# Rope rotation, key halves and tail norms moved from TensorE to VectorE and ScalarE in a two-block fp32 kernel

## The chip, the cores and the metric

One Trainium2 chip, one core. The metric is the device time of one launch in microseconds (us). Three runs of the kernel before gave a median of 1538.11 us (1537.73 to 1539.76).

## What is computed

The reference is a stack of two blocks on a sequence of 256 rows, D = 1024, in fp32. The first block has feed-forward layers, a recurrent mixer and a spatial gating mixer. The second block has two hybrid layers; each one computes projections of the normed input, sliding-window attention with 16 heads of 64 channels (two key heads, 16 meta tokens, so L = 272), and an mLSTM. The change lies in the attention's queries and keys:

```python
def rms_norm_2(x, g):
    y = xf * lax.rsqrt(jnp.mean(xf * xf, axis=-1, keepdims=True) + EPS)
    return (y * g.astype(jnp.float32)).astype(x.dtype)

def apply_partial_rope(x, cos, sin):
    half = ROT_DIM // 2                                   # ROT_DIM = 16
    x1, x2, rest = x[..., :half], x[..., half:ROT_DIM], x[..., ROT_DIM:]
    out = jnp.concatenate([x1 * c - x2 * s, x2 * c + x1 * s, rest], axis=-1)
...
scores = jnp.einsum('bnqkgd,bnskd->bnkgqs', qb, kb) * scale    # q, k normed per head, then rotated
e = jnp.exp(scores - m)
probs = e / (e.sum(axis=-1, keepdims=True) + jnp.exp(sink_b - m))
```

## The kernel before

Five instruction streams are written by hand, one for each engine, and run in the order in which they are written; semaphores tie them together.

**Weights.** The weights stream through in units of up to four 128x256 blocks in a ring of four slots. For each unit SyncE starts a load of 512 KB into `raw`, ScalarE makes `w_hi` (line 951, a rounded copy), VectorE makes `w_lo = raw - w_hi` (line 1478), and TensorE runs three products for each block (lines 541 to 543: hi·hi, hi·lo, lo·hi) on two output tiles, so 24 matmuls for a unit. `split_w(U + 3)` stands at unit U in ScalarE's and VectorE's streams: weights are made three units ahead. `w_hi` of unit U can be written once TensorE has finished unit U - 4. VectorE then takes each output tile from its bank with `scaled` (line 1518).

**Attention between the units.** In each hybrid layer the steps of the attention are hung on units by the table `VISITS`: TensorE does them after the unit of that number, VectorE and GpSimd at the same place in their streams. The phases are kv (units 0, 1), mif (2, 3), aq (4 to 11), mqk (12 to 19), and then the rest. The steps that matter here:

- `turn(c)`, c = 0 for the keys and 1 to 8 for the query chunks (two heads of 64 channels in the 128 partitions), at unit 5 (c = 0) and two each at units 7, 9, 11 and 13. ScalarE squares the chunk (line 1159). GpSimd multiplies it by sine and cosine tables (lines 1439 and 1440; `qs`, `qc`, two buffers each). TensorE sums the squares by head (line 733, into bank 4) and rotates `qs` with the matrix `rot_g` (line 738, into bank 5 or 6). VectorE adds that bank to `qc` (line 1842). `turn_mm` is raised by line 738, and ScalarE's next squares and VectorE's addition wait for it.
- `rs` at unit 14: VectorE turns the sums of squares into reciprocal roots (lines 1832 to 1835, `norms`), a chain of small steps that ends with `rs_new`.
- `rt` at units 15 and 16: TensorE waits for `rs_new`, transposes `norms` (line 757), ScalarE copies it to `r_t`, TensorE spreads it by one-hot matrices over the partitions of each head (line 747 for the keys, line 750 for the last 16 rows of eight chunks). VectorE scales the keys (line 1848) and the tail queries (line 1851, into `q_tail`).
- `kx` at unit 17: TensorE swaps the two key halves of 64 partitions by a matrix (line 763), transposes the values (765) and gate rows (770). ScalarE copies the swapped halves to `k_swap` and `k_up` (1168, 1169), VectorE the unswapped half and the values (1860 to 1867).
- `att` from unit 18: one head a visit. Line 801 is the first score matmul (the tail item of a key head), and it waits for all that `kx` made.

Matmuls of plain fp32 operands (lines 733 to 763) run in two passes, and so the profile has two records for each.

Of the kernel before, what the change touches and what calls it, by code (L numbers as in the profile page):

```python
# [38 lines left out]
CONST_W = dict(ident=P, tri=P, amask=AW, tmask=L, mmask=P, rot=P, swap=P, head_mean=2, cos=L, sin=L, sel=(NC8 + 1) * P)  # L39
# [8 lines left out]
def constants():  # L48
# [13 lines left out]
    for h0 in (0, DH):  # L62
        for d in range(half):
            c["rot"][h0 + half + d, h0 + d] = -1
            c["rot"][h0 + d, h0 + half + d] = 1
    c["swap"][i, (i + DH) % P] = 1
# [4 lines left out]
    for h0 in (0, DH):  # L71
        for k in (0, half):
            c["cos"][h0 + k:h0 + k + half] = np.cos(ang)
            c["sin"][h0 + k:h0 + k + half] = np.sin(ang)
    for k in range(NC8 + 1):
        for e in range(2):
            c["sel"][2 * k + e, k * P + e * DH:k * P + (e + 1) * DH] = 1
# [15 lines left out]


# [77 lines left out]
def build_stack(nc: bass.Bass, consts, x, ffn1_norm, ffn1_w_in, ffn1_w_out, mix_norm, ffn2_norm, ffn2_w_in, ffn2_w_out,  # L172
# [12 lines left out]
    with ExitStack() as ctx:  # L185
# [80 lines left out]
        rot_g = region(2, P)  # L266
# [1893 lines left out]
```

## Time and profile before

| | us |
|---|---|
| median of three runs | 1538.11 |
| the profiled execution | 1541.56 |
| its span in the trace | 1539.8 |
| TensorE busy | 1488.7 (97%) |
| VectorE busy | 1050.3 (68%) |
| ScalarE busy | 768.7 (50%) |
| GpSimd busy | 293.7 (19%) |

All times below are microseconds from the span's start. Layer 0's `turn` to `kx` lies between 980 and 1042, layer 1's between 1269 and 1329. The profiled execution lies 3.45 us above the median of the timed runs.

### The profile page before, as it was taken

The page shows a single profiled execution, that of the slowest core. Times are in us where ns is not written, and L with a number is a line of the kernel's source. Part 1 is how long each engine was busy: PE and PEld are TensorE (multiplying, and loading weights), DVE is VectorE, ACT ScalarE, POOL GpSimd, SP SyncE. Part 2 cuts the span into 40 slices and gives each one's busy share as a digit, 9 for nine tenths or more (in the row PEclk, how much of TensorE's full clock was granted, in tenths as well). Part 3 has the DMA queues.
Part 4 walks back from the last instruction along what each step waited for, and adds up shares of the span by engine and source line. Part 5 has one row for each costly group of instructions (what it writes and reads, how often), then busy time and mean ns, then how long its engine had stood idle before and what let it go on. Part 6 is the DMA issues. An engine that isn't in the chain of part 4 may idle for free.

```text
span 1539.8 us, 31458 instructions
## 1 busy us (share of the span) xinstructions
PE 1488.7 (97%) x11949; PEld 1467.5 (95%) x11949; DVE 1050.3 (68%) x2004; ACT 768.7 (50%) x1276; POOL 293.7 (19%) x361
## 2 busy tenths in 40 slices
PE   7999998999999999999999998999999999999998
PEld 7999998999999999999999997899999999899898
DVE  6666578766655666557766655888768768976883
ACT  5444458554545554454554534446744453566442
POOL 4111112211111111113311112343200125331000
PEclk9999999999999999999999999899999999999999
DMA  6656744555555655555565554443333554334333
GB/s 203 188 177 199 243 161 132 164 182 176 184 175 185 191 178 179 170 184 165 163 188 176 179 180 126 126 120 97 97 111 109 164 139 137 101 106 117 109 121 121
DMA packets 245276, 239.66 MB, mean 156 GB/s; under 512 B 15160, under 2 KB 244392, under 8 KB 245048
## 3 DMA queue, kind: packets, MB, share of 16 engines
q1 hardware_dynamic: 245176, 238.29, 50.8%
q8 instruction: 67, 1.10, 0.3%
q14 instruction: 33, 0.27, 0.1%
HBM read 237.21 MB, written 1.05 MB: 155 GB/s over the span
## 4 chain that ended last, share of the span: by engine, by line
PE 85%; DVE 10%; ACT 2%; issue 2%; POOL 1%; DMA 0%; SPq 0%; DVEq 0%; ACTq 0%; POOLq 0%
PE bank L541 25%; PE bank L543 25%; PE bank L542 25%; DVE w_lo L1478 3%; PE bank L865 1%; PE bank L805 1%; PE bank L823 1%; PE bank L788 1%; ACT w_hi L951 1%; DVE work L1518 1%; DVE work L1633 1%; PE bank L871 1%; PE bank L881 1%; PE bank L804 0%; DVE rstd L1496 0%
## 5 line engine op out<-in xcount | busy, mean ns | idle before, releaser
L1478 DVE TENSOR_TENSOR w_lo<-raw,w_hi 128x1024 fp32r<-128x1024 f32 (+1 forms) x456 | 557.7, 1232 | 317.8 <-ACT w_hi L951 317.4
L541 PE MATMUL bank<-x_hi,w_hi 128*128 128x256 f32 (+1 forms) x2480 | 721.8, 291 | 7.1 <-DVE x_lo L1491 5.2
L543 PE MATMUL bank<-x_hi,w_lo 128*128 128x256 f32 (+1 forms) x2480 | 708.8, 286 | 0.0
L542 PE MATMUL bank<-x_lo,w_hi 128*128 128x256 f32 (+1 forms) x2480 | 708.3, 286 | 0.0
L951 ACT CAST w_hi<-raw 128x1024 fp32r<-128x1024 f32 (+1 forms) x456 | 466.2, 1031 | 273.5 <-PE bank L543 256.8
L541 PEld LDWEIGHTS bank<-x_hi,w_hi 128*128 128x128 f32 x2480 | 477.9, 193 | 10.3 <-issue 6.8
L542 PEld LDWEIGHTS bank<-x_lo,w_hi 128*128 128x128 f32 x2480 | 478.2, 193 | 1.0
L543 PEld LDWEIGHTS bank<-x_hi,w_lo 128*128 128x128 f32 x2480 | 477.5, 193 | 0.0
L541 PE MATMUL bank<-y_hi,w_hi 128*128 128x256 f32 (+1 forms) x1088 | 310.4, 285 | 8.4 <-DVE y_lo L1489 8.3
L543 PE MATMUL bank<-y_hi,w_lo 128*128 128x256 f32 (+1 forms) x1088 | 309.8, 285 | 0.0
L542 PE MATMUL bank<-y_lo,w_hi 128*128 128x256 f32 (+1 forms) x1088 | 309.7, 285 | 0.0
L541 PEld LDWEIGHTS bank<-y_hi,w_hi 128*128 128x128 f32 x1088 | 209.3, 192 | 9.4 <-DVE w_lo L1478 4.4
L543 PEld LDWEIGHTS bank<-y_hi,w_lo 128*128 128x128 f32 x1088 | 209.4, 193 | 0.0
L542 PEld LDWEIGHTS bank<-y_lo,w_hi 128*128 128x128 f32 x1088 | 209.2, 192 | 0.0
L1353 POOL TENSOR_TENSOR work<-work,rstd 128x256 f32<-128x256 f32 x88 | 63.6, 742 | 415.1 <-ACT work L987 415.1
L1518 DVE TENSOR_TENSOR work<-bank,rstd 128x256 f32<-128x256 f32 (+1 forms) x204 | 81.7, 422 | 17.1 <-PE bank L543 16.7
L997 ACT CAST y_hi<-work 128x256 f32 (+1 forms) x88 | 35.6, 408 | 90.3 <-DVE work L1534 90.2
L987 ACT ACTIVATE work<-work 128x256 f32<-128x256 f32 x88 | 36.1, 419 | 78.3 <-DVE work L1518 78.3
L1334 POOL TENSOR_TENSOR sq<-h 128x256 f32<-128x256 f32 (+1 forms) x48 | 33.5, 698 | 199.2 <-DVE h L1563 196.9
L958 ACT ACTIVATE x_hi<-h,par 128x256 fp32r<-128x256 f32 (+1 forms) x64 | 32.8, 514 | 70.2 <-DVE h L1563 62.7
L1491 DVE SCALAR_TENSOR_TENSOR x_lo<-h,par,x_hi 128x256 fp32r<-128x256 f32 (+1 forms) x64 | 36.3, 569 | 29.9 <-ACT x_hi L958 29.8
L1332 POOL TENSOR_TENSOR sumsq<-h 128x256 f32<-128x256 f32 (+1 forms) x8 | 4.9, 618 | 248.1 <-DVE h L1563 240.8
(269 smaller groups left out, 1250.4 us busy)
## 6 DMA issues: line engine op xcount, KB each, us to landing
raw<-in_ffn_w_in_dram SPq DMA_DIRECT2D x176, 512.0 KB, 3.7
raw<-in_w_in_dram SPq DMA_DIRECT2D x100, 512.0 KB, 3.6
raw<-in_ffn_w_out_dram SPq DMA_DIRECT2D x64, 512.0 KB, 4.2
raw<-in_w_out_dram SPq DMA_DIRECT2D x32, 512.0 KB, 3.8
raw<-in_ffn_w_out_dram SPq DMA_DIRECT2D x32, 384.0 KB, 3.1
raw<-in_rec_w_in_dram SPq DMA_DIRECT2D x16, 512.0 KB, 3.6
raw<-in_sg_w_in_dram SPq DMA_DIRECT2D x16, 512.0 KB, 3.5
raw<-in_rec_w_out_dram SPq DMA_DIRECT2D x8, 512.0 KB, 3.4
```

Source lines behind the costliest of these rows:

```text
L541: mm(acc, wh, xh, start=first and j == 0, stop=False)
L542: mm(acc, wh, xl, start=False, stop=False)
L543: i_ = mm(acc, wl, xh, start=False, stop=last and j == n - 1)
L951: nc.scalar.copy(w_hi[:, s, 0:n, :], raw[:, s, 0:n, :]).then_inc(hi_made, 1)
L958: i_ = activation(xview(dst, k, N), src, ACT.Copy, scale=scale)
L987: activation(ffn_s[:, m, :], ffn_t[:, m, :], ACT.Silu).then_inc(silu_done, 1)
L997: nc.scalar.copy(dst, ffn_h[:, m, :]).then_inc(act_hi, 1)
L1334: link(TT(sq[:, T0:L], src(c), src(c), MUL))
L1353: TT(ffn_r[:, m, :], ffn_s[:, m, :], rstd[:, META:L], MUL).then_inc(gate_scaled, 1)
L1478: TT(w_lo[:, s, 0:n, :], raw[:, s, 0:n, :], w_hi[:, s, 0:n, :].bitcast(fp32), SUB).then_inc(lo_made, 1)
L1491: i_ = STT(out=xview(dst_lo, k, N), in0=src, scalar=scale, in1=hi, op0=MUL, op1=SUB)
L1518: TT(dst, tile(pr, m, N), rstd[:, T0:L], MUL).then_inc(tile_read, 1)
```

## The change

For the rotation, GpSimd multiplies by a sine table that now holds the head's gain, the scale and the sign (`sin_g`, made by VectorE as `cos_g` is); VectorE then permutes the partitions of `qs` in place within each group of 32 (`stream_shuffle`, with `ROPE_SWAP` exchanging 0 to 7 with 8 to 15) and adds `qc`. Line 738's matmul and the banks 5 and 6 fall away there; TensorE's `turn` no longer waits for GpSimd, and the last matmul of the head sums raises `turn_mm`. In `rt`, the eight matmuls with 16 columns become one with 18 (`tail_rows`), from which VectorE makes a column of norms for each tail row (`tail_t`, `tail_r`); the tail queries are copied unscaled, and the norm becomes the scale of the exponential. In `kx`, VectorE copies the key halves across partitions, and both the swap matmul and ScalarE's two copies fall away.

```diff
 turn, TensorE
-                        mm(bank[4][0:w, at:at + 2], score[:, n % 2, a:a + w], cst("head_mean"), start=True, stop=True)
-                    pe.wait_ge(qc_new, n + 1)
-                    pe.wait_ge(cos_ready, l + 1)
-                    if c >= 2:
-                        pe.wait_ge(q_ready, n - 1)
-                    mm(bank[5 + n % 2][:, 0:L], rot_g[:, 0 if c else 1, :], qs[:, n % 2, :], start=True,
-                       stop=True).then_inc(turn_mm, 1)
+                        i_ = mm(bank[4][0:w, at:at + 2], score[:, n % 2, a:a + w], cst("head_mean"), start=True, stop=True)
+                    i_.then_inc(turn_mm, 1)
 rt, TensorE
-                        mm(bank[6][:, 0:L], con[:, at:at + P], r_t, start=True, stop=True)
-                        for c in range(NC8):
-                            at = CONST_AT["sel"] + (c + 1) * P
-                            i_ = mm(bank[7][:, c * TAIL:(c + 1) * TAIL], con[:, at:at + P], r_t[:, 2 * P:L],
-                                    start=True, stop=True)
-                        i_.then_inc(rt_mm, 1)
+                        mm(bank[6][:, 0:L], cst("k_rows"), r_t, start=True, stop=True)
+                        mm(bank[7][:, 0:NR], cst("tail_rows"), norms[:, 3, 2 * NR:3 * NR], start=True,
+                           stop=True).then_inc(rt_mm, 1)
                         return
                     pe.wait_ge(rs_new, l + 1)
-                    pe.wait_ge(q_ready, 9 * (l + 1))
+                    if l:
+                        pe.wait_ge(m_sb, M_H * l)
 kx, TensorE and ScalarE
-                    pe.wait_ge(k_ready, l + 1)
-                    mm(bank[4][:, 0:L], cst("swap"), k_att, start=True, stop=True)
-                nc.scalar.copy(k_swap[DH:P, :], bank[4][DH:P, 0:L])
-                nc.scalar.copy(k_up[0:DH, 1, :], bank[4][0:DH, 0:L]).then_inc(k_swapped, 1)
 att, ScalarE
-                            i_ = activation(pr[:, 0:L], s[:, 0:L], ACT.Exp, bias=nm[:, 0:1], accum_out=den[:, 0:1])
+                            i_ = activation(pr[:, 0:L], s[:, 0:L], ACT.Exp, scale=tail_r[:, g:g + 1], bias=nm[:, 0:1],
+                                            accum_out=den[:, 0:1])
 turn, GpSimd
-                    TT(qs[:, n % 2, :], src, cst("sin"), MUL)
+                    TT(qs[:, n % 2, :], src, sin_g[:, 0 if c else 1, :], MUL).then_inc(qs_new, 1)
 tables, VectorE
-                    TS(rot_g[:, 0, :], cst("rot"), gq, sc, MUL, MUL)
-                    TS(rot_g[:, 1, :], cst("rot"), gk, None, MUL).then_inc(cos_ready, 1)
+                    TS(sin_g[:, 0, :], cst("sin"), gq, sc, MUL, MUL)
+                    TS(sin_g[:, 1, :], cst("sin"), gk, None, MUL).then_inc(cos_ready, 1)
 turn, VectorE
-                    dve.wait_ge(turn_mm, n + 1)
-                    TT(dst, bank[5 + n % 2][:, 0:L], qc[:, n % 2, :], ADD).then_inc(q_ready, 1)
+                    dve.wait_ge(qs_new, n + 1)
+                    link(V.stream_shuffle(qs[:, n % 2, :], qs[:, n % 2, :], ROPE_SWAP))
+                    dve.wait_ge(qc_new, n + 1)
+                    dve.wait_ge(qsq_new, n + 1)
+                    TT(dst, qs[:, n % 2, :], qc[:, n % 2, :], ADD).then_inc(q_ready, 1)
 rt, VectorE
                     dve.wait_ge(rt_mm, 2 * l + 2)
+                    dve.wait_ge(q_ready, 9 * (l + 1))
                     TT(k_att, k_att, bank[6][:, 0:L], MUL).then_inc(k_ready, 1)
+                    link(TT(tail_t, bank[7][:, 2:NR], cst("tail_head"), MUL))
+                    link(V.tensor_reduce(tail_r[:, 0:2], tail_t.rearrange("p (g n) -> p g n", g=2), mybir.AxisListType.X, ADD))
+                    TS(tail_r[:, 2:4], tail_r[:, 0:2], -1.0, None, MUL)
-                            i_ = TT(q_tail[...], q[...], bank[7][...], MUL)
+                            i_ = V.tensor_copy(q_tail[...], q[...])
 kx, VectorE
+                    dve.wait_ge(padded, l + 2)
+                    dve.wait_ge(k_ready, l + 1)
+                    V.tensor_copy(k_swap[DH:P, :], k_att[0:DH, :])
+                    V.tensor_copy(k_up[0:DH, 1, :], k_att[DH:P, :])
+                    link(V.tensor_copy(k_up[0:DH, 0, :], k_att[0:DH, :]))
+                    V.memset(k_att[0:DH, :], 0.0).then_inc(k_swapped, 1)
                     dve.wait_ge(kx_mm, l + 1)
-                    dve.wait_ge(padded, l + 2)
-                    V.tensor_copy(k_up[0:DH, 0, :], k_att[0:DH, :])
...
-                    link(i_)
-                    V.memset(k_att[0:DH, :], 0.0)
```

VectorE's stream at units 7 and 8 of layer 0 before (`w_lo` of a unit is line 1478, tiles are line 1518, line 1606 is a step of the mLSTM's gate logarithm, line 1842 is the rotation's addition for two query chunks):

```order
L1478 TENSOR_TENSOR w_lo<-raw,w_hi 128x1024 x2
L1518 TENSOR_TENSOR work<-bank2,rstd 128x272
L1518 TENSOR_TENSOR work<-bank3,rstd 128x272
L1606 SCALAR_TENSOR_TENSOR work<-work 4x272 x4
L1842 TENSOR_TENSOR work<-bank6,work 128x272
L1842 TENSOR_TENSOR work<-bank5,work 128x272
L1478 TENSOR_TENSOR w_lo<-raw,w_hi 128x1024 x2
```

The same place after the change (the line numbers are the changed kernel's):

```order
L1466 TENSOR_TENSOR w_lo<-raw,w_hi 128x1024 x2
L1506 TENSOR_TENSOR work<-bank2,rstd 128x272
L1506 TENSOR_TENSOR work<-bank3,rstd 128x272
L1594 SCALAR_TENSOR_TENSOR work<-work 4x272 x4
L1830 STREAM_SHUFFLE work<-work 128x272
L1833 TENSOR_TENSOR work<-work 128x272
L1830 STREAM_SHUFFLE work<-work 128x272
L1833 TENSOR_TENSOR work<-work 128x272
L1466 TENSOR_TENSOR w_lo<-raw,w_hi 128x1024 x2
```

Two shuffles have come in ahead of the next weights, and the additions read SBUF alone.

VectorE's stream from `rt` to the first item of the attention, before (line 1922 is the mLSTM's convolution):

```order
L1848 TENSOR_TENSOR work<-work,bank6 128x272
L1851 TENSOR_TENSOR work<-work,bank7 64x64 x4
L1478 TENSOR_TENSOR w_lo<-raw,w_hi 128x1024
L1518 TENSOR_TENSOR pre<-bank0,rstd 128x272
L1518 TENSOR_TENSOR pre<-bank1,rstd 128x272
L1922 SCALAR_TENSOR_TENSOR work<-pre,par,work 128x272 x6
L1860 COPY work<-work 64x272
L1862 COPY work<-bank5 128x2x64 x2
L1862 COPY work<-bank5 16x2x64
L1865 MEMSET work 64x272
L1866 COPY work<-bank5 128x16
L1867 COPY work<-bank5 16x8
```

And after:

```order
L1840 TENSOR_TENSOR work<-work,bank6 128x272
L1841 TENSOR_TENSOR work<-bank7,con 128x16
L1842 TENSOR_REDUCE work<-work 128x2
L1843 TENSOR_SCALAR work<-work 128x2
L1846 COPY work<-work 64x64 x4
L1466 TENSOR_TENSOR w_lo<-raw,w_hi 128x1024
L1506 TENSOR_TENSOR pre<-bank0,rstd 128x272
L1506 TENSOR_TENSOR pre<-bank1,rstd 128x272
L1918 SCALAR_TENSOR_TENSOR work<-pre,par,work 128x272 x6
L1854 COPY work<-work 64x272
L1855 COPY work<-work 64x272
L1856 COPY work<-work 64x272
```

Three small instructions stand in `rt` ahead of the tail copies, and two more copies of 64x272 stand in `kx` ahead of the value copies.

## Rows read from the trace of the kernel before

**Rows 1.** The page: busy time, share of the span, instructions.

```profile
PE 1488.7 (97%) x11949; PEld 1467.5 (95%) x11949; DVE 1050.3 (68%) x2004; ACT 768.7 (50%) x1276; POOL 293.7 (19%) x361
```

**Rows 2.** Waits of TensorE: line, releaser: us in total, times, longest.

```profile
PE bank L757 <- DVE work L1835: 3.7, 2, 1.9
PE bank L738 <- DVE work L1518: 1.9, 1, 1.9
PE bank L738 <- POOL work L1440: 1.9, 2, 1.6
PE bank L801 <- issue: 1.6, 2, 0.8
```

**Rows 3.** Timeline, TensorE: start, us, line, tile, count of records.

```profile
1000.01 0.71 PE L738 MATMUL bank<-work 128*128 128x272 f32 x2
1000.56 0.65 PE L733 MATMUL bank<-con,work 128*128 128x2 f32 x6
...
1318.20 1.85 PE L750 MATMUL bank<-work,con 128*128 128x16 f32 x16
```

**Rows 4.** Windows: us; busy PE, PEld, DVE, ACT, POOL; granted clock; DMA, GB/s.

```profile
986.20:1026.04 39.84, 36.50 (x263) 35.33 (x261) 32.40 (x64) 13.29 (x19) 21.20 (x20) 0.91 0.42 119
1026.04:1041.80 15.76, 14.89 (x104) 13.97 (x105) 13.36 (x32) 7.80 (x14) 5.04 (x6) 0.89 0.35 101
1275.90:1314.13 38.23, 34.10 (x260) 32.93 (x259) 33.25 (x64) 13.09 (x19) 21.07 (x20) 0.96 0.43 125
1314.13:1328.40 14.27, 13.41 (x105) 12.52 (x105) 13.09 (x32) 7.80 (x14) 6.08 (x6) 1.00 0.39 110
1045.00:1140.00 95.00, 95.00 (x727) 92.32 (x726) 67.79 (x227) 58.87 (x160) 20.61 (x22) 1.00 0.39 111
```

**Rows 5.** Waits of VectorE between 986.20 and 1026.04.

```profile
DVE w_lo L1478 <- ACT w_hi L951: 5.5, 3, 3.6
DVE pre L1518 <- PE bank L543: 0.3, 1, 0.3
DVE work L1518 <- PE bank L543: 0.3, 1, 0.3
```

**Rows 6.** Waits of VectorE between 1275.90 and 1314.13.

```profile
DVE w_lo L1478 <- ACT w_hi L951: 3.4, 2, 2.1
```

**Rows 7.** Timeline of VectorE: single and linked operations of 272 elements.

```profile
1009.84 0.43 DVE L1823 TENSOR_TENSOR work<-work 4x272 f32<-4x272 f32 x1
1010.31 0.71 DVE L1824 TENSOR_TENSOR_SCAN work<-work 4x272 f32<-4x272 f32 x1
1011.73 0.77 DVE L1842 TENSOR_TENSOR work<-bank,work 128x272 f32<-128x272 f32 x2
1012.43 1.20 DVE L1478 TENSOR_TENSOR w_lo<-raw,w_hi 128x1024 fp32r<-128x1024 f32 x1
```

**Rows 8.** Timeline of VectorE: tables, weights beside GpSimd, `rt` and `kx`.

```profile
972.24 0.35 DVE L1793 TENSOR_SCALAR work<-con,par 128x272 f32<-128x272 f32 x1
972.50 0.36 DVE L1794 TENSOR_SCALAR work<-con,par 128x272 f32<-128x272 f32 x1
...
992.60 1.63 DVE L1478 TENSOR_TENSOR w_lo<-raw,w_hi 128x1024 fp32r<-128x1024 f32 x1
...
1033.52 0.44 DVE L1848 TENSOR_TENSOR work<-work,bank 128x272 f32<-128x272 f32 x1 [1.26 <-PE bank L750]
...
1040.36 0.28 DVE L1860 COPY work<-work 64x272 f32<-64x272 f32 x1
...
1041.59 0.14 DVE L1867 COPY work<-bank 16x8 f32<-16x8 f32 x1
```

**Rows 9.** Windows around pauses of TensorE; columns as in Rows 4.

```profile
989.50:996.30 6.80, 6.20 (x25) 5.97 (x26) 4.59 (x9) 0.86 (x2) 4.27 (x5) 0.50 0.62 173
1279.60:1283.00 3.40, 3.18 (x12) 2.95 (x13) 3.26 (x8) 0.78 (x2) 1.01 (x3) 0.50 0.83 256
1312.30:1314.20 1.90, 0.01 (x1) 0.02 (x2) 1.66 (x9) 0.00 (x0) 0.00 (x0) 1.00 0.17 58
1314.20:1318.00 3.80, 3.80 (x29) 3.52 (x30) 3.42 (x7) 2.33 (x4) 0.00 (x0) 1.00 0.41 110
```

More of the change, by code:

```diff
@@ L36 @@
 C_AQ, C_KV, C_AG, C_MQK, C_MV, C_MIF, C_MO, C_MG = 0, 1024, 1280, 2304, 3328, 4352, 4360, 5384
-CONST_W = dict(ident=P, tri=P, amask=AW, tmask=L, mmask=P, rot=P, swap=P, head_mean=2, cos=L, sin=L, sel=(NC8 + 1) * P)
+CONST_W = dict(ident=P, tri=P, amask=AW, tmask=L, mmask=P, head_mean=2, cos=L, sin=L, k_rows=P, tail_rows=P, tail_head=ATT_H)
 CONST_AT = {}
@@ L61, in constants @@
     half = ROT // 2
[L62 to L66, printed above, removed]
     c["head_mean"][i, i // DH] = 1.0 / DH
@@ L71, in constants @@
     for h0 in (0, DH):
-        for k in (0, half):
+        for k, sign in ((0, 1), (half, -1)):
             c["cos"][h0 + k:h0 + k + half] = np.cos(ang)
[L74 to L77, printed above, removed]
+            c["sin"][h0 + k:h0 + k + half] = sign * np.sin(ang)
+        c["k_rows"][h0 // DH, h0:h0 + DH] = 1
+    c["tail_rows"][i % TAIL, i] = 1
+    for g in range(2):
+        for j in range(4):
+            for e in range(2):
+                c["tail_head"][e * DH + j * TAIL:e * DH + (j + 1) * TAIL, 8 * g + 2 * j + e] = 1
     return np.concatenate([c[n] for n in CONST_W], 1)
@@ L92 @@
         _r += _k
+ROPE_SWAP = [*range(ROT // 2, ROT), *range(ROT // 2), *range(ROT, 32)]
 def plan():
@@ L265, in build_stack @@
         cos_g = region(2)
[L266 removed]
+        sin_g = region(2)
+        tail_r = region(1, 4)[:, 0]
+        tail_t = region(1, ATT_H)[:, 0]
         qsq = score[:, :, 0:L]
@@ L335, in build_stack @@
             sem(n) for n in ("ws_tr", "ws_read", "vt_tr", "vt_read", "sg_mm", "sg_read"))
-        cos_ready, qsq_new, qc_new, turn_mm, q_ready = (
-            sem(n) for n in ("cos_ready", "qsq_new", "qc_new", "turn_mm", "q_ready"))
+        cos_ready, qsq_new, qs_new, qc_new, turn_mm, q_ready = (
+            sem(n) for n in ("cos_ready", "qsq_new", "qs_new", "qc_new", "turn_mm", "q_ready"))
         rs_new, rt_mm, rt_read, k_ready, tail_new = (
@@ L1245, in nothing @@
                     return None
-                do = dict(turn=turn, rs=nothing, rt=lambda n: rt() if n == 0 else None, kx=lambda n: kx(), att=att,
+                do = dict(turn=turn, rs=nothing, rt=lambda n: rt() if n == 0 else None, kx=nothing, att=att,
                           silu=silu, mvt=mvt_chunk, ml=lambda hs: ml(*hs))
```

15 lines of the change are left out of this document (5 added, 10 removed).

## The prediction

> **What bounds the kernel now.** I read the busy times first: TensorE is busy 97% of the span [rows 1]. So matmuls that go away are worth their length, unless something else is late where they stood. The waits of TensorE name the places where something is: in the steps that the change touches it waits 3.8 us for what line 738 reads, 3.7 us ahead of `rt` for VectorE's root chain, and 1.6 us ahead of the first attention item [rows 2]. Then I cut the span into stages. In layer 0, from the first rotation's addition (986.2) to the end of the root chain (1026.04), TensorE has 36.5 us of work in 39.84 us and VectorE 32.4; in layer 1 it is 34.1 and 33.25 of 38.23 [rows 4]. The two engines are nearly even there, whereas in the attention that follows TensorE is busy all of 95 us and VectorE 68 [rows 4]. Both stretches end in one meeting point: TensorE's `rt` at unit 15 waits for `rs_new`, which VectorE raises at the end of a fixed stream. So the question of the first stretch is when VectorE gets there, not how much work TensorE has.
>
> **What TensorE sheds.** Line 738 takes 1000.56 - 1000.01 = 0.55 us until the next matmul can start, 18 of them 9.9 us; the sixteen 16-column records take 1.85 us and are replaced by two (0.23 us), twice, 3.2 us [rows 3]; the swap has line 738's form, at most 0.55 us, twice, 1.1 us. Together 14.2 us. Besides, the 3.8 us of waiting at line 738 go, and what followed them: the granted clock was 0.50, the 1.2 GHz level, for 6.8 us after the wait of 1.6 us in layer 0 and for 3.4 us after the 1.9 us in layer 1 [rows 2, 9], worth half of that, 5.1 us. That is 23.1 us in all, all of it ahead of the first attention item.
>
> **What VectorE takes on before `rs_new`.** Each of the nine chunks of a layer costs an addition now and a shuffle, a link and an addition after. A pair of unlinked additions lasts 0.77 us, 0.43 the single one, so 0.35 from start to start; a linked operation of 272 elements is followed after 1010.31 - 1009.84 = 0.47 us [rows 7]. No row is a shuffle. Its bounds: a one-source operation on 128x272 gives way after 0.26 us (972.24 to 972.50) [rows 8], with the link's 0.03 about 0.3 us; and 0.7 us if it is as long as the 0.47 of the linked operation, the two further waits cost something, and the addition, which now reads both inputs from SBUF, is stretched by GpSimd as line 1478 is (1.63 us beside it, 1.20 alone) [rows 7, 8]. I take 0.5 us, near the linked operation, since the operation is elementwise over the same 272. That is 4.5 us a layer. The two tables of 272 columns (0.26 us each) replace two of 128; I put the difference at 0.13 us a layer, half of one.
>
> By the Trainium skill, "VectorE: DVE Perf Modes", section "The perf-mode tier table", a stream shuffle has the 1x mode only, about 2400 ns for 2048 elements; an estimate from it is 0.32 us for 272. The Trainium skill, same page, section "The DRAIN you can't avoid", says that a semaphore after each operation costs nothing over none; the rows have 0.47 linked against 0.35 unlinked. With that rule the shuffle and its addition would add about 0.35 instead of 0.5 a chunk, and the whole result would be 2.7 us lower, 1539.2.
>
> **The first stretch.** How much can VectorE be pulled forward? Only by the time it now waits for others: 6.1 us in layer 0 [rows 5] and 3.4 us in layer 1 [rows 6]; almost all of it is for `w_hi`, which waits for a slot that TensorE frees. With TensorE ahead these waits go. So `rs_new` of layer 0 comes 6.1 - 4.5 - 0.13 = 1.5 us earlier, and that of layer 1 4.5 + 0.13 - 3.4 = 1.2 us later. TensorE meanwhile has, in layer 0, 36.5 us of work less 3.4 for the slow clock and 5.0 for nine matmuls, 28 us of a stretch of 38.3: it arrives some 10 us early at unit 15 and stands idle, and what it shed turns into a wait for VectorE at `rt`. GpSimd's part stays as it is; the chunk after next waits for `q_ready`, but VectorE comes back only two units later, and GpSimd needs 21 us of the 39 for all nine [rows 4].
>
> **From `rs_new` to the first item.** Behind `rs_new` VectorE has a fixed stream too: `w_lo`, tiles, convolution, `w_lo`, `rt`, `w_lo`, tiles, convolution, `kx`. In layer 0 it idles 1.26 us in it, for line 750 [rows 8]; the new `rt` needs TensorE 1.6 us less, so this goes. In layer 1 it is busy 13.09 of 14.27 us and has no such wait [rows 4]. Added: in `rt` a 16-column multiply, a reduction and a scalar step, all linked, about 0.15 us each (estimated from the small copy of 0.14 us [rows 8]), 0.45 us; in `kx` two more copies of 64x272 at 0.28 us each [rows 8], 0.55 us. So +1.0 us a layer, -1.3 in layer 0. ScalarE's two copies were beside other work and give nothing; the swap's matmul and the shorter `rt` lie in front of a wait and give nothing more. Layer 0: -0.3. Layer 1: +1.0.
>
> **The clock.** Now TensorE ends unit 18 about 15.0 us after `rs_new` in layer 0 and waits 0.8 us for the first item at 15.8 [rows 2, 4]. With `rt` 1.6 us and the swap some 0.5 us shorter it ends at 12.9, and the item can start at 15.5: a pause of 2.6 us. In layer 1 the same working gives 13.4 - 2.1 = 11.3 against 15.2, a pause of 3.9 us, or 2.2 if the clock was low behind `rt`. Pauses of 1.6 and 1.9 us ahead of line 738 were followed by 0.50 for 6.8 and 3.4 us; the one of 1.9 us ahead of line 757 in layer 1 was not (1.00 after it) [rows 2, 9]. A pause of 2.2 us or more is longer than all of these, so I take a period of 3.4 us at 1.2 GHz after it, 1.7 us, in each layer: +3.4 us. What follows is TensorE's own work [rows 4], so it counts in full. The ten idle microseconds ahead of `rt` will bring a slow period too. VectorE has 6.2 us of its own work between `rs_new` and `rt` (two weights, two tiles and a convolution), and TensorE at full clock needs some 4.3 for a unit and both halves of `rt`: a period of 3.4 us is hidden, one of 6.8 us (3.4 us lost) costs some 1.2 us a layer.
>
> **The sum**, against the profiled execution of 1541.56 us (span 1539.8, and 3.45 above the median): -1.5 + 1.2 - 0.3 + 1.0 + 3.4 = +3.8 us. On the median that is **1541.9 us**.
>
> **The rivals.**
> *The work comes off.* If VectorE has more room than its waits show, TensorE's 23.1 us come off, less the 3.4 us of the slow periods above and the 1.5 us in `rt` and `kx`: about 1520. For it speaks the share of TensorE in the whole span; against it that `rt` already waits for VectorE by 1.8 us in each layer before anything is shed. 7 in 100. Half-way, if the chunks cost 0.3 and the clock stays, -3.6 - 3.4 + 3.8 = -3.2, 1534.9, or somewhat below: 15 in 100.
> *No slow period ahead of the attention.* Then the sum is +0.4, 1538.5. The row of layer 1's `rt` speaks for it. Together with the case of cheap shuffles and slow periods (+0.2): 32 in 100.
> *VectorE and GpSimd stretch each other.* The mechanism: both inputs of the new addition come from SBUF, and the first chunk's `q_ready` sets GpSimd going on the next one while VectorE shuffles and adds the second. At 0.7 us a chunk `rs_new` comes 1.8 us later in each layer, +3.6 more, 1545.5; with slow periods of 6.8 us behind `rt` 1548. It is slower than before from 0.55 us a chunk on even if only one slow period comes. 16 in 100.
> *My forecast*, 1540 to 1544: 30 in 100.
>
> **How the numbers follow.** The likeliest is the forecast and gives the time. The range takes in the cheap end with the clock kept (1534.9, a little below) and the dear end (1548): 1534 to 1548. Left out is the case of the work coming off and the tails, about 15 in 100. Within 0.2% is 3.1 us to either side, about what a measurement here can tell: faster 0.18, same 0.36, slower 0.46; the forecast lies only 0.7 us beyond the bound, so a part of it counts as the same.
>
> **What would show it.** In the changed profile: TensorE's wait at the first transposes of `rt` is 8 to 11 us in both layers, on VectorE; VectorE's waits for `w_hi` between the first rotation and `rs_new` are close to none; from a shuffle's start to the next `w_lo` a pair takes about 1.7 us; the stretch corresponding to 986.20:1026.04 is about 38.3 us long, and layer 1's about 39.3; the wait ahead of the first item is 2.2 to 3.9 us, and the granted clock is 0.50 behind it. I am wrong if VectorE still waits for `w_hi` there, if the wait at `rt` is short, or if a shuffle takes far from 0.43 us.

## Result and profile after

The change makes the kernel slower: 1557.23 us (median of four, 1555.11 to 1557.53) against 1537.92 in the same session, a ratio of 1.0117 with a 95% interval of 1.0103 to 1.0132. The forecast was 1541.9 with a range of 1534 to 1548. Its sign and the two places where TensorE now waits for VectorE were right; the rise on the median was five times what was forecast (19.1 us for 3.8), because VectorE's added work was priced too low.

The page of the changed kernel (as [rows 1]; the span is 1555.5): TensorE is busy 8.5 us less, VectorE 19.3 more.

```profile
PE 1480.2 (95%) x11881; PEld 1459.5 (94%) x11881; DVE 1069.6 (69%) x2050; ACT 765.9 (49%) x1272; POOL 299.5 (19%) x361
```

TensorE's waits (line, releaser: us in total, times, longest), as [rows 2]. Line 752 is the first transpose of `rt`, 794 the first attention item, 544 the weight matmuls with `w_lo`.

```profile
PE bank L752 <- DVE work L1823: 19.1, 2, 9.5
PE bank L794 <- DVE work L1857: 8.6, 2, 4.6
...
PE bank L544 <- DVE w_lo L1466: 7.4, 5, 2.1
```

All three are VectorE's. The 3.8 us at the rotation's matmul [rows 2] are gone; these three have 15.4, 7.0 and 5.6 us more than before, 28 us in all (the wait for `w_lo` was 1.8). Of the waits for `w_lo` 5.0 us lie in the changed steps, 2.1 in layer 0 and 2.9 in layer 1.

Windows from the first shuffle to the end of the root chain in layers 0 and 1, then from there to the first attention item, as [rows 4] (us; busy PE, PEld, DVE, ACT, POOL; granted clock; DMA, GB/s):

```profile
988.00:1028.97 40.97, 29.37 (x242) 28.93 (x240) 39.22 (x81) 12.57 (x19) 24.16 (x20) 0.91 0.40 116
1283.99:1324.88 40.89, 28.50 (x238) 27.84 (x237) 39.15 (x81) 12.32 (x19) 24.20 (x20) 0.92 0.40 117
1028.97:1047.03 18.06, 14.03 (x88) 13.05 (x89) 15.94 (x37) 7.13 (x12) 6.74 (x8) 0.78 0.31 88
1324.88:1342.57 17.69, 12.99 (x89) 12.02 (x89) 16.44 (x37) 7.09 (x12) 6.79 (x8) 0.89 0.32 90
```

VectorE is busy 39.2 of 41 us where it was 32.4 of 39.8 and 33.3 of 38.2 [rows 4]. The time stands in this table, in us from each execution's trace. **B** goes from the layer's first head-sum matmul to the end of the root chain (`rs_new`), **C** from there to the first attention item; the columns between hold the rest.

| | start | B, layer 0 | C, layer 0 | to layer 1 | B, layer 1 | C, layer 1 | rest |
|---|---|---|---|---|---|---|---|
| before | 979.67 | 46.37 | 15.78 | 227.59 | 44.72 | 14.24 | 211.43 |
| the change | 981.30 | 47.67 | 18.06 | 230.27 | 47.58 | 17.69 | 212.93 |
| difference | +1.6 | +1.3 | +2.3 | +2.7 | +2.9 | +3.5 | +1.5 |

The differences add up to 15.7 us. One pair of chunks shows where B's come from. First VectorE's timeline in the changed kernel (1830 is the shuffle, 1833 the addition, 1466 `w_lo`, 1506 takes a tile from its bank), then GpSimd's products of the same moment:

```profile
994.26 0.46 DVE L1830 STREAM_SHUFFLE work<-work 128x272 f32<-128x272 f32 x1
994.75 0.44 DVE L1833 TENSOR_TENSOR work<-work 128x272 f32<-128x272 f32 x1
...
995.12 0.46 DVE L1830 STREAM_SHUFFLE work<-work 128x272 f32<-128x272 f32 x1
995.61 0.78 DVE L1833 TENSOR_TENSOR work<-work 128x272 f32<-128x272 f32 x1
996.32 3.50 DVE L1466 TENSOR_TENSOR w_lo<-raw,w_hi 128x1024 fp32r<-128x1024 f32 x2
999.75 0.77 DVE L1506 TENSOR_TENSOR work<-bank,rstd 128x272 f32<-128x272 f32 x2
```

```profile
995.34 0.76 POOL L1427 TENSOR_TENSOR work<-work 128x272 f32<-128x272 f32 x1 [2.92 <-DVE work L1833]
996.06 0.97 POOL L1428 TENSOR_TENSOR work<-work 128x272 f32<-128x272 f32 x1
996.99 1.75 POOL L1427 TENSOR_TENSOR work<-work 128x272 f32<-128x272 f32 x1
998.71 1.75 POOL L1428 TENSOR_TENSOR work<-work 128x272 f32<-128x272 f32 x1
```

The first addition has 0.44 us. It raises `q_ready` and lets GpSimd go. The second addition is issued at 995.61, in the middle of GpSimd's first product, and ends 0.34 us later than it would alone. Then the engines alternate, as worked out from these rows: GpSimd's second product ends at 997.03, the first `w_lo` about 1.04 us later (996.32 and half of 3.50), GpSimd's third at 998.74, the second `w_lo` 1.08 us after that (999.82), GpSimd's fourth 0.64 us later. Each runs while the other stands, and each record includes the standing. The shuffle beside GpSimd (995.12) and the tiles with one input from a bank (999.75) keep their lengths. `w_lo` goes from 1.41 and 1.45 us in the mean to 1.67 in both layers, ten times in each. Its group in the stretch from the first rotation to `rs_new` (total us and mean ns behind the bar, then VectorE's idle time in front of it), before and after, layer 0:

```profile
L1478 DVE TENSOR_TENSOR w_lo<-raw,w_hi 128x1024 fp32r<-128x1024 f32 x10 | 14.0, 1405 | 5.5 <-ACT w_hi L951 5.5
L1466 DVE TENSOR_TENSOR w_lo<-raw,w_hi 128x1024 fp32r<-128x1024 f32 x10 | 16.4, 1673 | 0.0
```

In C the same happens to copies. VectorE in the changed kernel, in layer 0 and (the last two lines) in layer 1: 1843 to 1846 belong to `rt`, 1854 to 1857 to `kx`; in layer 0 GpSimd runs products from 1034.17 to 1038.23 and from 1044.04 to 1047.30.

```profile
1036.81 0.60 DVE L1843 TENSOR_SCALAR work<-work 128x2 f32<-128x2 f32 x1
1037.32 1.39 DVE L1846 COPY work<-work 64x64 f32<-64x64 f32 x4
...
1043.94 0.30 DVE L1854 COPY work<-work 64x272 f32<-64x272 f32 x1
1044.25 0.76 DVE L1855 COPY work<-work 64x272 f32<-64x272 f32 x1
1045.03 0.82 DVE L1856 COPY work<-work 64x272 f32<-64x272 f32 x1
1045.96 0.28 DVE L1857 MEMSET work<- 64x272 f32 x1
...
1331.76 0.17 DVE L1843 TENSOR_SCALAR work<-work 128x2 f32<-128x2 f32 x1
1331.84 2.41 DVE L1846 COPY work<-work 64x64 f32<-64x64 f32 x4
```

The copy that starts ahead of GpSimd lasts 0.30 us, the next two 0.76 and 0.82. A step of two columns takes 0.60 us beside GpSimd (layer 0) and 0.17 alone (layer 1).

The pauses of TensorE in layer 0, from its timeline:

```profile
1029.03 0.72 PE L752 MATMUL bank<-con,work 128*18 128x128 f32 x3 [9.54 <-DVE work L1823]
...
1047.03 1.25 PE L794 MATMUL bank<-work 128*128 128x272 f32 x2 [3.98 <-DVE work L1857]
```

And the granted clock behind them, the third figure from the end, in windows of the changed kernel:

```profile
1030.00:1040.00 10.00, 10.00 (x63) 9.67 (x62) 8.57 (x20) 4.22 (x7) 3.90 (x4) 0.74 0.38 107
1040.00:1050.00 10.00, 6.02 (x35) 5.60 (x35) 7.99 (x21) 3.80 (x9) 3.10 (x4) 0.77 0.19 53
1047.03:1050.00 2.97, 2.97 (x11) 2.74 (x12) 1.65 (x4) 0.89 (x4) 0.27 (x1) 0.50 0.00 0
1050.00:1060.00 10.00, 10.00 (x71) 9.88 (x70) 7.30 (x23) 4.89 (x12) 1.75 (x2) 0.89 0.37 107
```

### The profile page after: what moved, and what is told of

The parts are those of the page before. It is cut to its first block, busy times and chain, and to the rows that moved or that the text cites. A ratio compares the mean times of both kernels' runs of the same rounds, so it can differ in the third digit from the quotient of the medians.

```text
span 1555.5 us, 31363 instructions
## 1 busy us (share of the span) xinstructions
PE 1480.2 (95%) x11881; PEld 1459.5 (94%) x11881; DVE 1069.6 (69%) x2050; ACT 765.9 (49%) x1272; POOL 299.5 (19%) x361
## 4 chain that ended last, share of the span: by engine, by line
PE 80%; DVE 14%; issue 2%; ACT 2%; POOL 0%; DMA 0%; SPq 0%; DVEq 0%; ACTq 0%; POOLq 0%
PE bank L544 24%; PE bank L546 24%; PE bank L545 24%; DVE w_lo L1466 4%; PE bank L858 1%; DVE work L1506 1%; PE bank L798 1%; PE bank L816 1%; DVE work L1918 1%; PE bank L781 1%; DVE work L1621 1%; ACT w_hi L944 1%; PE bank L864 1%; PE bank L874 1%; DVE work L1830 1%
```

## The experiments

Stages of each, in the columns of the table above:

| | start | B0 | C0 | to layer 1 | B1 | C1 | rest | ratio to before (95%) |
|---|---|---|---|---|---|---|---|---|
| rope alone | 979.21 | 47.69 | 16.68 | 227.81 | 47.60 | 15.81 | 211.30 | 1.0061 (1.0044 to 1.0078) |
| `kx` alone | 979.61 | 43.57 | 15.97 | 229.10 | 44.55 | 17.51 | 212.79 | 1.0036 (1.0022 to 1.0051) |
| tail norms alone | 980.64 | 45.12 | 15.94 | 229.16 | 44.49 | 15.93 | 212.82 | 1.0045 (1.0028 to 1.0062) |
| no shuffle | 980.22 | 43.75 | 17.67 | 230.63 | 42.95 | 17.73 | 213.65 | 1.0055 (1.0038 to 1.0072) |
| pauses filled | 980.88 | 47.67 | 17.67 | 227.87 | 47.58 | 17.68 | 211.35 | 1.0101 (1.0084 to 1.0117) |
| GpSimd 34 wide | 979.19 | 43.01 | 17.68 | 229.35 | 42.92 | 17.68 | 212.87 | 1.0042 (1.0026 to 1.0059) |
| `kx` on ScalarE | 979.39 | 47.66 | 16.38 | 229.42 | 47.54 | 16.02 | 212.89 | 1.0089 (1.0072 to 1.0106) |
| `qs` alone waited for | 979.73 | 42.37 | 15.78 | 227.56 | 42.18 | 14.24 | 211.54 | 0.9975 (0.9965 to 0.9985) |
| conv. behind norms | 980.97 | 43.36 | 22.21 | 229.18 | 43.26 | 22.20 | 213.72 | 1.0110 (1.0095 to 1.0125) |
| `qs` and conv. | 979.41 | 38.84 | 21.05 | 227.57 | 38.64 | 21.09 | 211.60 | 1.0011 (1.0002 to 1.0020) |
| GpSimd later | 980.08 | 47.12 | 17.70 | 230.64 | 47.08 | 17.73 | 212.95 | 1.0101 (1.0086 to 1.0117) |
| `qs`, GpSimd later | 980.78 | 44.10 | 15.76 | 227.60 | 43.87 | 15.78 | 211.51 | 1.0001 (0.9992 to 1.0010) |

The rows "no shuffle", "pauses filled", "GpSimd 34 wide", "`kx` on ScalarE", "conv. behind norms" and "GpSimd later" are edits of the changed kernel (itself 1.0117); the others are edits of the kernel before. A ratio of 0.001 is 1.5 us. The stages come from one profiled execution of each kernel, the ratios from all its runs.

### One part at a time

The rotation alone (its three hunks of the diff on the kernel before):

> The kernel before with the rotation alone moved to VectorE; tail norms and key halves stay on TensorE. Theory A (the VectorE stream ahead of rs_new is the path, and GpSimd lengthens it): most of the loss is here, +8 to +13 us over the kernel before, with a wait of 8 to 10 us at the first transposes of rt in both layers. Theory B (the key copies and the tail steps behind rs_new are the larger part): +2 to +5 us.

The key halves alone (`kx` hunks):

> The kernel before with the key halves alone copied by VectorE. Theory A: +3 to +5 us, as the two added copies take 0.76 and 0.82 us beside GpSimd in place of 0.28, in each layer, and the longer pause ahead of the first item brings a slow clock. Theory B (copies cost only what one alone costs): +1 us.

The tail norms alone (`rt` and exponential hunks):

> The kernel before with the tail norms alone changed: one matmul of 18 columns for eight of 16, unscaled copies, the norm as the exponential's scale. Theory A: VectorE gives back in layer 1 what TensorE saves in layer 0, -1 to +2 us. Theory B (TensorE's work comes off): -3 us.

The ratios say 9.4, 5.5 and 6.9 us (0.0061, 0.0036 and 0.0045 of 1540), 22 together; the change has 18. No part is worth having. The rotation's 9.4 us lie in the range of theory A, 5.5 us for `kx` a little above it. The rotation alone lengthens B to the change's own length in both layers, with TensorE waiting 9.5 and 8.1 us at `rt`. The tail norms missed both theories (-1 to +2, or -3): they take 1.6 us off TensorE ahead of `kx` and the first item comes no sooner. TensorE's waits between 1015 and 1055 in this kernel:

```profile
PE bank L803 <- issue: 4.1, 1, 4.1
PE bank L759 <- DVE work L1838: 1.8, 1, 1.8
```

In layer 0 the item started 15.78 us after `rs_new` before and starts 15.94 after it now, since VectorE sets it: its last copy of `kx` ends at 1041.60 and the item starts at 1041.70 (in layer 1, where it was 14.24, it is 15.93: the four copies of 64x64 last 2.40 us beside GpSimd, the multiplications lasted 0.92); TensorE only stands 4.1 us instead of 0.8, and the granted clock of 1040 to 1050 goes from 1.00 to 0.83, so that the stage behind it costs 1.6 and the last one 1.4 us more. `kx` alone has pauses of 3.0 us there and the same +1.5 and +1.4.

### The shuffle left out

```diff
-                    link(V.stream_shuffle(qs[:, n % 2, :], qs[:, n % 2, :], ROPE_SWAP))
```

> The changed kernel without the stream shuffle and its link (the sine products are added unpermuted, so the rotation is left out). The shuffle takes 0.46 us, 18 of them 8.3 us. If the VectorE stream sets the time of rs_new one for one and GpSimd's share is independent: 7 to 9 us faster than the changed kernel. If GpSimd's collision with the w_lo steps is what counts: 2 to 4 us faster only, with the two w_lo steps of a visit still at 3.5 us.

B shrinks by 3.92 and 4.63 us, 0.44 and 0.51 a chunk: the shuffle costs what its record says (0.458) and its link little. The ratio falls by 0.0062, 9.5 us, a little more than the 7 to 9 of the first theory. The pair of `w_lo` keeps its 3.50 us, so the hold is a cost of its own. B1, at 42.95, is 0.8 us longer than where TensorE's rotation doesn't wait (42.18), though TensorE has no rotation to do; likely this is the hold on additions and `w_lo`.

### The pauses filled

```diff
+                    for _ in range(15):
+                        mm(bank[6][:, 0:L], ident, x_hi[:, 0:L].bitcast(fp32), start=True, stop=True)
                     pe.wait_ge(rs_new, l + 1)
...
+                            for _ in range(6):
+                                mm(bank[4][:, 0:L], ident, x_hi[:, 0:L].bitcast(fp32), start=True, stop=True)
                             pe.wait_ge(k_swapped, l + 1)
```

> The change, with 15 extra fp32 matmuls of 272 columns in TensorE's stream ahead of its wait for rs_new and 6 ahead of its wait for att0's keys, in both layers; their results go into banks nobody reads. They only keep the array at work in the pauses (9.5 us ahead of rs_new, 4 to 4.6 us ahead of att0); all that is computed stays. Theory 'clock': the change's cost over its waits comes from the periods at 1.2 GHz that follow these pauses (granted clock 0.56 to 0.83 in 1020 to 1060 and 1310 to 1350); with the array busy they go, the stretch behind rs_new comes down from 18.1 and 17.7 us to about 16.5, att0 to the next layer's first norm matmul and to the end lose 1.5 to 2.5 us each, and the time falls by 5 to 9 us, to about 1548 to 1552, with mean clock at 0.99 instead of 0.981. Rival 'order': the clock only follows; VectorE's chain is the end in both places, so filling changes under 2 us (1555 to 1559). If the extra matmuls outlast a pause, the time rises instead and the chain of waits shows a shorter or no wait there.

Half right. The stages behind the items fall to the level of before (227.87 and 211.35), 2.40 and 1.58 us less than in the change: that is what the slow clock costs there. B doesn't move at all and C by 0.4 us, in layer 0 alone, so ahead of the items the slow clock costs next to nothing; it is VectorE that is late. (In layer 0 VectorE's wait of 0.86 us ahead of `rt` is gone too, but its steps there fall elsewhere against GpSimd's products, and the four copies of 64x64 take 2.40 us instead of 1.39.) The time fell by 2.5 us (0.0016 by the ratios), under the 5 to 9 expected; the 4.0 us of the two stages are from the fastest of its executions.

### GpSimd's products at 34 columns

```diff
-                    TT(qs[:, n % 2, :], src, sin_g[:, 0 if c else 1, :], MUL).then_inc(qs_new, 1)
+                    W = L if c < 2 else 34
+                    TT(qs[:, n % 2, 0:W], src[:, 0:W], sin_g[:, 0 if c else 1, 0:W], MUL).then_inc(qs_new, 1)
```

and the same for `qc`.

> The change, with GpSimd's two rotation products of chunks 2 to 8 made 34 columns wide instead of 272 (the other columns keep what the buffers held, so the rotated queries are not the reference's); VectorE's shuffles, additions, halves w_lo and all matmuls are as in the change. Theory 'GpSimd stretches VectorE': the second addition of a pair falls from 0.78 to about 0.44 us, the pair of w_lo from 3.50 to 2.4 to 2.8 us, a pair of chunks costs about 1.3 us less, four pairs 4 to 5 us a layer: first shuffle to rs_new 36 to 37 us instead of 41, TensorE's wait there 9.5 us falls to about 5, and the time falls by 8 to 12 us to about 1545 to 1549. Rival 'shuffle's own length and its links': additions and w_lo keep their lengths or VectorE waits for something else (w_hi, or the squares), and the time falls by less than 3 us.

VectorE's and GpSimd's timelines of this kernel, one pair:

```profile
999.98 0.50 DVE L1834 TENSOR_TENSOR work<-work 128x272 f32<-128x272 f32 x1
1000.40 2.41 DVE L1467 TENSOR_TENSOR w_lo<-raw,w_hi 128x1024 fp32r<-128x1024 f32 x2
```

```profile
999.70 0.26 POOL L1428 TENSOR_TENSOR work<-work 128x34 f32<-128x34 f32 x1 [3.75 <-DVE work L1834]
...
1000.62 1.11 POOL L1428 TENSOR_TENSOR work<-work 128x34 f32<-128x34 f32 x1 [0.44 <-DVE work L1834]
1001.69 1.24 POOL L1429 TENSOR_TENSOR work<-work 128x34 f32<-128x34 f32 x1
```

The pair of `w_lo` is back at 2.41 us, and a product of 34 columns that takes 0.26 us alone takes 1.11 beside a `w_lo`: now GpSimd is the one held. B falls by 4.66 us in each layer, and the ratio from 1.0117 to 1.0042, which is 11.5 us: both as expected. So of the change's cost in time more than half is VectorE standing while GpSimd works, with the clock behind it. TensorE's wait at `rt` is 7.3 and 8.3 us, not the 5 expected: its waits for `w_lo` in B (2.1 us in layer 0, 2.9 in layer 1) are gone too, so it comes earlier.

### The key halves copied by ScalarE

```diff
+                    nc.scalar.copy(k_swap[DH:P, :], k_att[0:DH, :])
+                    nc.scalar.copy(k_up[0:DH, 1, :], k_att[DH:P, :]).then_inc(k_swapped, 1)
...
-                    V.tensor_copy(k_swap[DH:P, :], k_att[0:DH, :])
-                    V.tensor_copy(k_up[0:DH, 1, :], k_att[DH:P, :])
```

> The change, with the two copies that make the swapped key halves moved from VectorE to ScalarE, straight from k_att (no swap matmul); the clearing of k_att waits for them. Theory 'VectorE's chain sets att0': rs_new to att0 is VectorE's own stream in the change (TensorE waits 4.0 and 4.6 us there); without the copies of 0.76 and 0.82 us it ends 1.3 to 1.7 us earlier in each layer, TensorE's pause falls to about 2.5 us, and with the clock the time falls by 3 to 6 us, to about 1551 to 1554. Rival 'shed work is the pause': the same stretch is set by something else (gate exponentials, w_hi), the pause stays at 4 us and the time moves by under 1.5 us. Third way: the copies on ScalarE delay w_hi there and att0 comes no sooner.

C falls by 1.68 and 1.67 us: the two copies' own length (0.30 and 0.76) and what the third was held, which falls from 0.82 to 0.29. VectorE's stream sets the first item. The ratio falls by 0.0028, 4.3 us, as expected.

### The first convolutions behind the norms

```diff
-                                if ph == "mqk":
+                                if ph == "mqk" and p:
                                     conv(p)
...
+                            if u == 14:
+                                conv(0)
```

> The change, with one edit of VectorE's order: the first pair of convolutions (six instructions of 128x272, 3.6 us where they stand, 12 scheduling groups before the attention) is done right behind the norms that raise rs_new instead of ahead of the last two rotation additions; nothing is computed otherwise. Theory 'VectorE's own stream sets rs_new, TensorE is only early': rs_new comes 2.9 to 3.6 us earlier in each layer, TensorE's wait there falls from 9.5 to about 6 us; but the convolutions then stand in the stretch from rs_new to att0, which VectorE sets too, so that this grows by as much (from 18.1 and 17.7 us to 20.5 to 21.5), TensorE's pause ahead of att0 grows from 4 to 4.6 us to 6 or more, and the time stays within 3 us of 1557. Rival 'only the wait at rs_new matters': rs_new to att0 stays at about 18 us and the time falls by 5 to 8 us.

B falls by 4.3 us in both layers, C rises by 4.2 and 4.5, and the ratio is 1.0110 for 1.0117. The gain in B was larger than the 2.9 to 3.6 expected, and so was the loss in C. TensorE's two waits in layer 0 become 5.23 and 6.93 us instead of 9.54 and 3.98, with one of 1.65 between them:

```profile
1024.39 0.72 PE L752 MATMUL bank<-con,work 128*18 128x128 f32 x3 [5.23 <-DVE work L1823]
...
1046.54 1.25 PE L794 MATMUL bank<-work 128*128 128x272 f32 x2 [6.93 <-DVE work L1857]
```

So B and C are one stretch of VectorE's stream, of 65.3 to 65.7 us, with TensorE waiting at two places in it. This other order of it gains nothing.

### GpSimd's products moved behind `w_lo`

```diff
                         pool.wait_ge(q_ready, n - 1)
+                    if c in (3, 5, 7):
+                        pool.wait_ge(lo_made, PHASES[f"kv{l}"][0] + 7 + 2 * ((c - 1) // 2) + LEAD + 1)
```

> The change, with one wait more on GpSimd: the rotation products of chunks 3, 5 and 7 (and behind them 4, 6 and 8) begin only when VectorE has made the second w_lo behind the additions. All work is kept. Theory 'VectorE is held while a GpSimd instruction runs at the same moment': in the three pairs the second addition falls from 0.78 to 0.44 us and the pair of w_lo from 3.50 to about 2.4, 1.4 us a pair, 4 us a layer, less what GpSimd's four products of 0.76 us now take from the small two-input steps that follow (three to five of 0.43 us) and from the next shuffle, which may wait for them: rs_new 1 to 4 us earlier in each layer and the time 3 to 10 us lower, 1547 to 1554. Rival 'GpSimd's work as such': the stretch moves to other instructions one for one and the time stays within 2 us of 1557; or VectorE waits for qs and qc and it rises.

VectorE's timeline of this kernel, then that of the change at the same work:

```profile
994.39 0.44 DVE L1835 TENSOR_TENSOR work<-work 128x272 f32<-128x272 f32 x1
994.75 2.35 DVE L1468 TENSOR_TENSOR w_lo<-raw,w_hi 128x1024 fp32r<-128x1024 f32 x2
997.02 0.78 DVE L1508 TENSOR_TENSOR work<-bank,rstd 128x272 f32<-128x272 f32 x2
997.72 2.48 DVE L1596 SCALAR_TENSOR_TENSOR work<-work 4x272 f32<-4x272 f32 x3
1000.23 0.90 DVE L1598 SCALAR_TENSOR_TENSOR work<-work 4x272 f32<-4x272 f32 x1
```

```profile
1000.45 1.35 DVE L1594 SCALAR_TENSOR_TENSOR work<-work 4x272 f32<-4x272 f32 x3
1001.83 0.43 DVE L1596 SCALAR_TENSOR_TENSOR work<-work 4x272 f32<-4x272 f32 x1
```

The addition and the pair of `w_lo` are back at 0.44 and 2.35 us, 1.5 us less; but three steps on 4 partitions go from 1.35 to 2.48 and the next from 0.43 to 0.90, 1.6 us more. B is 0.5 us shorter, the ratio 1.0101. That the hold follows the time of GpSimd's products was right; the gain I expected was not. The steps on 4 partitions, which stand beside the products now, are held too: this is the rival, the stretch moves to other instructions one for one.

### The kernel before, with TensorE waiting for what it reads

In the kernel before, line 738 reads `qs` but waited for `qc`, which GpSimd finishes one product later.

```diff
-                    pe.wait_ge(qc_new, n + 1)
+                    pe.wait_ge(qs_new, n + 1)
...
-                    TT(qs[:, n % 2, :], src, cst("sin"), MUL)
+                    TT(qs[:, n % 2, :], src, cst("sin"), MUL).then_inc(qs_new, 1)
...
+                    dve.wait_ge(qc_new, n + 1)
                     dve.wait_ge(turn_mm, n + 1)
```

> The kernel before, with one edit: TensorE's rotation matmul waits for qs alone (the operand that it reads), and the addition on VectorE waits for qc; before, TensorE waited for qc, which GpSimd makes 0.8 to 1.7 us after qs. All of the work stays on TensorE. Theory: the two waits of 1.9 us each on the rotation's line and the slow period behind them go or shrink, TensorE is released 0.8 us earlier at each chunk, and the time falls by 2 to 5 us to 1533 to 1537. Rival: VectorE's stream sets rs_new anyway; what TensorE gains there it waits longer for rs_new (3.7 us in all before), and the time stays within 1 us of 1538, or rises by 1 to 2 us where the longer pause brings a slow period.

The same kernel once more:

> The kernel before with TensorE's rotation matmul waiting for qs alone, once more beside the run above, on the same chip, in five rounds, since the first time gave a ratio of 0.9975 with its interval from 0.9965 to 0.9985. Expected again: 0.9965 to 0.9985, which is 2.3 to 5.4 us faster. If the first was chance, the interval will hold 1.

The ratios are 0.9975 and 0.9979 (0.9969 to 0.9989): 3.2 to 3.9 us faster than before, and the fastest kernel of the study (medians 1535.85 and 1535.49). TensorE's waits of this kernel:

```profile
PE bank L757 <- DVE work L1835: 4.3, 2, 2.1
...
PE bank L738 <- POOL work L1439: 0.9, 4, 0.3
```

What is left at the rotation is 0.9 us of 3.8. B is 42.37 and 42.18; VectorE still waits 1.4 us for `w_hi` in layer 0. The gain in B is read best against `kx` alone, whose steps in B are those of before and whose B of layer 0 has no slow period: 43.57 and 44.55, so 1.2 and 2.4 us, which is the gain in time.

With the convolutions moved as well:

> The kernel before with the edit of the run that lets TensorE's rotation matmul wait for qs alone, and with the same reordering of the first convolutions behind the norms. Theory: TensorE's two waits of 2.1 us for rs_new go or fall under 0.5 us and with them the slow clock behind (0.83 in 1020 to 1030); TensorE needs 15.7 us of its own work from there to att0 and VectorE's stream, now 2.9 us longer there, ends about 1 to 3 us behind it instead of 0.8, so the gain is partly given back: 1532 to 1537. Rival: all of it is given back at att0, with a pause of 3 us and a slow period: 1536 to 1540.

B falls to 38.84 and 38.64, C rises by 5.3 and 6.9 us, more than was gained: the spreading matmul now waits 2.6 us in each layer for ScalarE's copy of the norms, which stands behind ScalarE's wait for VectorE's late tiles. The rival was nearer; at 1541.26 us the kernel is slower than before.

```profile
PE bank L747 <- ACT work L1163: 5.1, 2, 2.6
```

With GpSimd's products behind `w_lo`:

> The kernel before with TensorE's rotation matmul waiting for qs alone, and with GpSimd's products of chunks 3 to 8 behind the second w_lo as in the run above. If the hold cost the kernel before too, w_lo falls from 1.4 to about 1.25 us in the mean and rs_new comes up to 2 us earlier, and the time is 1 to 4 us below 1535.7. Rival: TensorE now waits for qs at the rotation of the next pair, which GpSimd starts later, and the time is 1 to 6 us above 1535.7.

The rival again: 1540.51 us. TensorE waits 3.2 us in nine pieces for the products, B grows by 1.7 us in both layers and C of layer 1 by 1.5.

## Why the prediction failed in size

**Held.** Both meeting points are VectorE's. The wait at `rt` is 9.5 us in both layers (8 to 11 forecast), VectorE's waits for `w_hi` between the first rotation and `rs_new` are gone, a shuffle takes 0.458 us (0.43), and what TensorE shed became waiting. A pause stands ahead of the first item, of 4.0 and 4.6 us, a little above the 2.2 to 3.9, with the low clock behind it (0.50 from 1047.03 to 1050 in layer 0): worth 2.40 and 1.58 us by the filled run, against 1.7 each. Two other signs missed, both to the dear side: a pair takes 2.06 us from its first shuffle to the next `w_lo` (1.7), and the stretches are 41.0 and 40.9 us long (38.3 and 39.3).

**The chunk's price, 0.5 us.** This is the step that failed. With VectorE's idle time taken off, 39.84 - 6.1 = 33.7 us in layer 0 became 40.97, and 38.23 - 3.4 = 34.8 became 40.89: 7.2 and 6.1 us for nine chunks, 0.80 and 0.67 each. In layer 0 that is beyond even the dear bound of 0.7. A shuffle with its link takes 0.49 us (988.00 to 988.49), so nine of them are 4.4 us and use up the 0.5 a chunk alone. The bound allowed for a hold on the new addition. It left out that `w_lo` would be held more often, which is 2.7 and 2.2 us (ten times 1.67 for 1.41 and 1.45). I counted VectorE's waits for `w_hi` [rows 5, 6] as room to move into, but in part of that room GpSimd had its products to itself (994.82 to 996.20 in layer 0 before, while VectorE waited from 994.2 to 997.8), as these rows of the kernel before show. A wait that hides another engine's use of a shared path isn't free. This gave `rs_new` +1.3 and +2.9 us in B for the -1.5 and +1.2 forecast: 4.5 us of the miss. The rival of the two engines stretching each other had the mechanism, with 16 in 100, and named the addition alone.

```profile
994.82 0.66 POOL L1439 TENSOR_TENSOR work<-work,con 128x272 f32<-128x272 f32 x1
995.44 0.76 POOL L1440 TENSOR_TENSOR work<-work 128x272 f32<-128x272 f32 x1
997.83 1.23 DVE L1478 TENSOR_TENSOR w_lo<-raw,w_hi 128x1024 fp32r<-128x1024 f32 x1 [3.60 <-ACT w_hi L951]
```

The Trainium skill states it in "SBUF — State Buffer", section "Who interferes with whom": VectorE's second SBUF input and its two-port copies go through a path shared with GpSimd, the one that comes first holds it for its whole instruction, and an instruction with at most one SBUF input, outside the two-port modes, isn't concerned. This case's trace agrees: 0.78 us for 0.44 for the addition, 0.76 and 0.82 for 0.30 for the copies, 1.11 for 0.26 on GpSimd, 0.46 unchanged for the shuffle. That `w_lo` is held could be read from the rows ahead of the change (1.63 us beside GpSimd for 1.20 [rows 7, 8]). Of the shuffle, "VectorE: DVE Perf Modes", section "The perf-mode tier table" of the Trainium skill, gave the estimate of 0.32 us; the trace has 0.458, and the measurement decides.

**`rt` and `kx`, 1.0 us a layer.** The steps of `rt`, from the scaling of the keys to the next `w_lo`, took 1.31 us before and 2.70 and 3.28 after; those of `kx`, from the first copy to the item, 1.46 and 1.49 before and 3.09 after. That is 3.0 and 3.6 us instead of 1.0, since copies were priced at 0.28 us from a row that starts while GpSimd stands still [rows 8]. In layer 0 the wait of 1.26 us that I let go stayed at 0.86: TensorE came to `rt`'s second half through a slow period (0.56 granted from 1029.03 to 1036.04) that I had called hidden in part, and with the pauses filled (0.78 from 1029 to 1036) the wait is gone. C is +2.3 and +3.5 us for the -0.3 and +1.0 forecast, 5.1 us of the miss.

**The rest.** 0.8 us are the size of the slow periods behind the items. 1.6 us arise ahead of the changed steps, where the clock was granted 0.66 from 950 to 970 against 0.74 before; no run shows that it is the change's doing: the other kernels start anywhere from 978.95 to 981.30, and the one in which TensorE waits for `qs` alone at 979.73 and 978.95 in its two profiles. The last 3.45 us are the profiled execution of before lying above its median, carried over as if the changed kernel's would too; the change's own profiled execution, 1557.5 us, lies on its median. In B of layer 0 it has 46.37 us, where `kx` alone, with the same steps up to there and the same wait (1.56 us) at line 738, has 43.57. The clock of that kernel, in the window where [rows 9] has 0.50, and VectorE's waits for `w_hi` from there on to `rs_new`:

```profile
989.50:996.30 6.80, 6.26 (x48) 6.18 (x49) 5.86 (x10) 1.91 (x3) 4.37 (x5) 1.00 0.61 174
...
DVE w_lo L1473 <- ACT w_hi L949: 2.7, 3, 1.4
```

So the slow period of 6.8 us is not in every execution. It is about 2.8 of the 3.45 us, and the changed kernel had no such excess to lose. It also made the room that the prediction counted on in layer 0: VectorE's waits for `w_hi` are 2.7 us without it, and not 5.5. Measured from 43.57, the change lengthens B of layer 0 by 4.1 us and not by 1.3.

4.5 + 5.1 + 0.8 + 1.6 = 12.0 us, and with 3.45 it is 15.5, for the 15.3 between forecast and result.

## What to carry to other kernels

Where VectorE and GpSimd work at the same time, price each added VectorE instruction with two SBUF inputs, or an fp32 SBUF copy, with the GpSimd instruction that may stand in its way, and price its neighbours again too; idle time of VectorE in which GpSimd works is not room. Work taken off the busiest engine was worth nothing in a stretch that another engine's stream sets, and the pause that it left cost clock behind it. Before room is counted from one profiled execution, a second one is worth a look: a slow period in the first can make most of it. The cheap gain was to look at which operand a wait is for: a matmul that waited for the second of two products, and read only the first.

## What the runs showed of the hardware

- Where VectorE reads two tensors from SBUF, or makes a copy or a scalar step on one there in fp32, VectorE and GpSimd took turns by whole instructions: two `w_lo` of 128x1024 in 3.50 us beside GpSimd's products, 2.35 with GpSimd later; a copy of 64x272 in 0.76 to 0.82 us, 0.30 alone; three steps on 4x272 in 2.48, 1.35 alone; a scalar step on 128x2 in 0.60, 0.17 alone; GpSimd's 128x34 product in 1.11, 0.26 alone. Not concerned: the stream shuffle (448 to 465 ns in all 18), and operations with one of two inputs from a bank (a pair of tiles 0.77 us beside GpSimd and 0.78 without it).
- A stream shuffle of 128x272 in fp32 takes 0.458 us; its mask load shows as 0.01.
- Four copies of 64x64 took 1.39 us in one layer and 2.41 in the other, by where GpSimd's products fell.
- After pauses of TensorE of 2.2 to 5.0 us ahead of the first item, the stages behind it were 1.4 to 3.1 us longer than before. They were back at the level of before with the array kept at work in part of the pause (2.0 us of it left), and in the rotation alone, which has pauses of 9.5 and 8.1 us ahead of `rt` but only 0.6 ahead of the item.
- A wait of 1.6 us of TensorE at the same place was followed by 6.8 us at a granted clock of 0.50 in one profile and by 1.00 in another.
